# Statistics per token in four layer norms, one projection panel in each of them, and decay rows added on VectorE

## What is computed

```python
def _layer_norm(x, g, b):
    mu = jnp.mean(x, -1, keepdims=True)
    var = jnp.mean(jnp.square(x - mu), -1, keepdims=True)
    return (x - mu) * lax.rsqrt(var + NORM_EPS) * g + b

# _fox_attend, for 16 heads of layer 1 (log_f = log_sigmoid of a projection)
c = jnp.cumsum(log_f, axis=1)
s = einsum(q, k) * d ** -0.5 + c[query] - c[key]      # then causal mask, softmax, times v

# first_block, per layer i of 2
x = _layer_norm(DN_ALPHA * x + m, ln1_g[i], ln1_b[i])
x = _layer_norm(DN_ALPHA * x + _sq_relu_mlp(x, w_up[i], w_down[i]), ln2_g[i], ln2_b[i])
gate = jax.nn.sigmoid(x @ ple_w_gate[i] + ple_b_gate[i])
x = x + gate * (p[i] @ ple_w_proj[i])
```

## Time and profile before

| | us |
|---|---|
| median of 3 runs (lowest to highest) | 2610.25 (2610.14 to 2611.8) |
| the profiled execution, its own time | 2608.08 |
| its span, first to last instruction | 2606.2 |
| PE busy | 2520.6 (97%) |
| DVE, POOL, ACT busy | 1314.6, 1159.6, 923.9 |

### The profile page before, as it was taken

How to read it: one execution, slowest core, us unless ns; L and a number is a source line. 1 busy time by engine, 2 the same in 40 slices (tenths; PEclk the granted TensorE clock), 3 DMA queues, 4 the chain that set the end, 5 groups by cost and what they waited for, 6 DMA issues and landing times.

```text
span 2606.2 us, 47076 instructions
## 1 busy us (share of the span) xinstructions
PE 2520.6 (97%) x18452; PEld 2062.2 (79%) x18452; DVE 1314.6 (50%) x1952; ACT 923.9 (35%) x1479; POOL 1159.6 (44%) x688
## 2 busy tenths in 40 slices
PE   8899899999999998999999999999999999999997
PEld 6677688887787876888877888888888878788886
DVE  3655864346414258543466655566658873321113
ACT  4433422223623234222235333333345563432221
POOL 4444544444544445444445323333247744444442
PEclk9999999999999999999999999999999999999999
DMA  6211232232231212333322111111113223232331
GB/s 176 84 41 48 82 97 97 90 101 83 81 97 31 67 49 81 97 97 97 97 81 87 58 35 35 50 35 43 35 52 97 97 82 104 92 102 91 95 101 53
DMA packets 57721, 203.19 MB, mean 78 GB/s; under 512 B 6448, under 2 KB 9176, under 8 KB 57560
## 3 DMA queue, kind: packets, MB, share of 16 engines
q1 hardware_dynamic: 54288, 196.37, 23.5%
q10 hardware_dynamic: 2920, 3.44, 0.8%
q0 software_dynamic: 352, 1.05, 0.1%
HBM read 197.17 MB, written 3.67 MB: 77 GB/s over the span
## 4 chain that ended last, share of the span: by engine, by line
PE 89%; DVE 5%; ACT 2%; issue 1%; POOL 1%; DMA 0%; SPq 0%; DVEq 0%; ACTq 0%; POOLq 0%
PE banks L1936 24%; PE banks L1938 24%; PE banks L1937 24%; PE banks L2383 9%; PE banks L2151 1%; PE banks L2433 1%; PE banks L2134 1%; POOL sb_pa L1823 1%; DVE sb_x L1149 1%; PE banks L2069 1%; PE banks L2112 1%; PE banks L2108 1%; PE banks L2293 1%; ACT sb_pa L629 1%; PE banks L2284 1%
## 5 line engine op out<-in xcount | busy, mean ns | idle before, releaser
L1797 POOL TENSOR_TENSOR sb_wl<-sb_raw,sb_wh 128x1024 fp32r<-128x1024 f32 (+1 forms) x366 | 882.0, 2413 | 1052.8 <-ACT sb_wh L472 1052.5
L1936 PE MATMUL banks<-sb_bh,sb_wh 128*128 128x512 f32 x2656 | 1052.8, 396 | 47.4 <-POOL sb_bl L1809 24.0
L1938 PE MATMUL banks<-sb_bh,sb_wl 128*128 128x512 f32 x2656 | 1040.4, 392 | 0.0
L1937 PE MATMUL banks<-sb_bl,sb_wh 128*128 128x512 f32 x2656 | 1040.3, 392 | 0.0
L1936 PEld LDWEIGHTS banks<-sb_bh,sb_wh 128*128 128x128 f32 x2656 | 501.2, 189 | 173.0 <-issue 46.9
L1938 PEld LDWEIGHTS banks<-sb_bh,sb_wl 128*128 128x128 f32 x2656 | 500.9, 189 | 108.7
L1937 PEld LDWEIGHTS banks<-sb_bl,sb_wh 128*128 128x128 f32 x2656 | 501.5, 189 | 106.9 <-issue 2.2
L472 ACT CAST sb_wh<-sb_raw 128x1024 fp32r<-128x1024 f32 (+1 forms) x366 | 376.5, 1031 | 465.4 <-PE banks L1938 462.5
L2383 PEld LDWEIGHTS banks<-sb_m 64*64 64x64 f32 x5632 | 195.7, 134 | 16.6 <-issue 7.7
L1069 DVE SCALAR_TENSOR_TENSOR sb_x<-sb_x,banks 128x512 f32 x72 | 49.5, 687 | 314.9 <-PE banks L1938 314.9
L2383 PE MATMUL banks<-sb_m 64*64 64x64 f32 (+1 forms) x5632 | 206.7, 229 | 0.5 <-DVE sb_w L1586 0.2
(11 more groups left out here) (344 smaller groups left out, 2640.6 us busy)
## 6 DMA issues: line engine op xcount, KB each, us to landing
sb_raw<-w SPq DMA_DIRECT2D x366, 512.0 KB, 3.5
sb_x<-xT SPq DMA_DIRECT2D x4, 512.0 KB, 6.8
out<-sb_x SPq DMA_DIRECT2D x4, 512.0 KB, 2.6
bias_rows<-sb_brow ACTq DMA_DIRECT2D x1, 1536.0 KB
sb_pj<-pT POOLq DMA_DIRECT2D x2, 512.0 KB, 4.0
sb_t<-bias_rows ACTq DMA_DIRECT2D x1, 512.0 KB, 3.7
sb_sq<-bias_rows ACTq DMA_DIRECT2D x1, 512.0 KB, 4.7
sb_wm<-wm ACTq DMA_DIRECT2D x1, 288.0 KB, 3.0
```

Of the source, the lines that this page charges most:

```text
L1797: nc.gpsimd.tensor_tensor(wl[:, s, 0:cols], raw[:, s, 0:cols], wh[:, s, 0:cols].bitcast(F32), ALU.subtract).then_inc(lo_ready, 1)
L1936: nc.tensor.matmul(out, hi_a, hi_b, start=first, stop=False)
L1937: nc.tensor.matmul(out, hi_a, lo_b, start=False, stop=False)
L1938: return nc.tensor.matmul(out, lo_a, hi_b, start=False, stop=last)
```

## The change

**Norms.** The sums over channels are no longer spread over partitions. `tokens` puts 128 tokens at a time in the stationary place against two columns of ones, so each statistic comes out as one number per token, tokens on the partitions (128x2 for each of four token blocks). Mean, variance, root and reciprocal are computed on 8 or 16 columns. `along_tokens` brings mean and inverse root back to rows of 512 in banks 2 and 3 by products with the identity. A dummy root on ACT stands ahead of the real one. DVE subtracts the mean from x and writes the scaled chunk into a ring of PSUM banks 4 to 7. ACT adds the bias from there, once for the high part and once for x. Low parts of even chunks are now made by DVE (`low`), those of odd chunks by POOL (`norm_odd`). `filled_norm` puts one p projection panel (24 matmuls) into every norm, and `arriving` with two panels follows in norm 2 too. p is fetched after the attention and split in the output projection ahead of norm 1 (`ple_high`, `ple_low`).

**Decay.** The decay rows go to DRAM and come back spread over 128 partitions, 8 heads at a time (2 MB on ACT's queue, twice). The products with `fc_h` and `fc_l` are gone. DVE adds the row to the scores in place and takes the maximum in the same operation, negated; the exponential gets scale -1. The fetch of `fsel` and POOL's wait for it are gone.

The core of the diff:

```diff
-                dve.wait_ge(ln_dsq, w.ln + 1)
-                dve.wait_ge(ln_ss, w.ln + 1)
-                nc.vector.tensor_tensor(s1, psum[:, 3, :], sd, ALU.subtract).then_inc(ln_var, 1)
+                def scaled_x(c):
+                    if c >= 4:
+                        dve.wait_ge(nhi_ready, n0 + (c - 4 if c % 2 else c - 2))
+                    dve.wait_ge(ln_sub, m0 + c + 1)
+                    nc.vector.scalar_tensor_tensor(psum[:, 4 + c % 4, :], x[:, c, :], pcol(*gcol(c)), psum[:, 3, :],
+                                                   ALU.mult, ALU.mult).then_inc(t_ready, 1)
+                def low(c):
+                    dve.wait_ge(ln_hi, NC // 2 * w.ln + c // 2 + 1)
+                    nc.vector.scalar_tensor_tensor(bl[0][:, c, :], psum[:, 4 + c % 4, :], pcol(*bcol(c)),
+                                                   bh[0][:, c, :].bitcast(F32), ALU.add, ALU.subtract).then_inc(ln_low_even, 1)
...
+                nc.vector.reciprocal(tok_inv, tok_sd).then_inc(ln_inv, 1)
+                dve.wait_ge(ln_mean_spread, w.ln + 1)
                 less_mean(0)
                 less_mean(1)
-                dve.wait_ge(sd_ready, w.ln + 1)
-                link(nc.vector.reciprocal(rs, sd))
...
+            def filled_norm(layer):
+                pe.wait_ge(pl_ready, layer + 1)
...
+                        if t == 0 and k == 0:
+                            pe.wait_ge(ln_mean, w.ln)
+                            along_tokens(2, tok_mean).then_inc(ln_mean_spread, 1)
...
+                    if t == 0:
+                        pe.wait_ge(ln_inv, w.ln)
+                        along_tokens(3, tok_inv).then_inc(ln_inv_spread, 1)
...
-                pe.wait_ge(pl_ready, layer + 1)
-                short(4, ph, pl, 2)
-                short(4, ph, pl, 2)
-                panels(NC, 0, ready=(opnd_pool, w.op))
+                filled_norm(layer)
+                arriving(0, even_and_odd(w.op))
+                panels(NC - 2, 0)
...
+                            nc.vector.tensor_tensor_reduce(s_i, s_i, decay[:, 2 * u + e, 0:width], -1.0, -NEG,
+                                                           ALU.add, ALU.min, nm[:, ring, e:e + 1]).then_inc(nm_ready, 1)
...
-                    if kind == "fox":
-                        for part_of in (fc_h, fc_l):
-                            for e in range(2):
-                                pick = fsel_r[rows[e], chunk0 + u:chunk0 + u + 1].broadcast_to([64, P])
-                                nc.tensor.matmul(out[e], pick, part_of[rows[e], k_c], start=False, stop=False)
```

More of the change, by code:

```diff
@@ L522, in stream_norm, with ring, high @@
                 act.wait_ge(ln_var, w.ln + 1)
-                nc.scalar.activation(sd, s1, ACT.Sqrt, bias=eps[:, 0:1]).then_inc(sd_ready, 1)
+                nc.scalar.activation(tok_sd, tok_var, ACT.Sqrt, bias=eps[:, 0:1]).then_inc(sd_ready, 1)
+                def ring(c):
+                    return psum[:, 4 + c % 4, :]
+                def high(c):
+                    act.wait_ge(t_ready, NC * w.norm + c + 1)
+                    ins = nc.scalar.activation(bh[0][:, c, :], ring(c), ACT.Identity, bias=pcol(*bcol(c)))
+                    if c % 2 == 0:
+                        ins.then_inc(ln_hi, 1)
@@ new lines, in whole @@
+                def whole(c):
+                    if c % 2 == 0:
+                        act.wait_ge(ln_low_even, NC // 2 * w.ln + c // 2 + 1)
+                    nc.scalar.activation(x[:, c, :], ring(c), ACT.Identity, bias=pcol(*bcol(c))).then_inc(nhi_ready, 1)
+                projected(q, 0)
+                high(0)
+                projected(q, 1)
+                high(1)
+                whole(1)
+                projected(q, 2)
+                projected(q, 3)
+                whole(0)
@@ L524, in stream_norm @@
+                for c in range(2, NC, 2):
+                    high(c)
+                    high(c + 1)
+                    whole(c + 1)
+                    whole(c)
                 w.ln += 1
                 w.norm += 1
[L526 to L539, removed]
+                w.mid += 3
+                w.p += 1
+                w.g += 4
             def rms_square(c, slot):
@@ L1943, in bank_wait, with in_order, even_and_odd, ready @@
                     pe.wait_ge(bank_free[b], g.over2())
+            def in_order(sema, base):
+                return lambda k: pe.wait_ge(sema, base + k + 1)
+            def even_and_odd(op):
+                def ready(k):
+                    if k % 2:
+                        pe.wait_ge(opnd_pool, op + k // 2 + 1)
+                    else:
+                        pe.wait_ge(ln_low_even, NC // 2 * (w.ln - 1) + k // 2 + 1)
+                return ready
             def arriving(bo, ready, sums=lambda: None):
-                for j in range(2):
-                    pe.wait_ge(lo_ready, w.p + j + 1)
-                    bank_wait((w.g + j) % 2, Idx(0, w.g + j))
                 for k in range(NC):
@@ L2084, in panels_and_sums, with tokens, along_tokens @@
                 w.ln += 1
+            def tokens(b, at_, rows):
+                for tb in range(NB):
+                    out = psum[:, b, at_ + 2 * tb:at_ + 2 * tb + 2]
+                    last = nc.tensor.matmul(out, rows[:, tb * P:tb * P + P], ones[:, 0:2], start=True, stop=True, skip_group_check=True)
+                return last
+            def along_tokens(b, factors):
+                for tb in range(NB):
+                    f = factors[:, 2 * tb:2 * tb + 1].broadcast_to([P, P])
+                    last = nc.tensor.matmul(psum[:, b, tb * P:tb * P + P], f, ident[:, :], start=True, stop=True, skip_group_check=True)
+                return last
```

187 lines of the change are left out of this document (113 added, 74 removed).

## The result

The changed kernel takes 2598.38 us (median of 5 runs, 2594.52 to 2600.35), the kernel before 2610.25 (5 runs beside them, 2609.92 to 2611.8). The ratio is 0.995, 95% interval 0.9938 to 0.9961: 11.9 us faster, half of the forecast 23.5. A second set of 5 runs gave 2598.8. The profiled execution took 2600.35 us, the slowest of the first five, with a span of 2598.5.

The account below looks back on a forecast made before the run. PE, busy 97% of the span, was taken as the bound. Norms 22.0, sigmoid wait -2.8 and decay +4.3 summed to 23.5 us, from 2608.1 to 2584.6, median 2587 us; bounds 2580 to 2593, range 2579 to 2600.

Parts of the forecast that it names:

- rival 1: Norms: PE's clock falls during the small two-column sums, costing 6 to 16 us; 2596 us, chance 0.14.
- the 22.8 us of a norm: Each norm, from first small sum to the end of `arriving`, takes 22.8 us; two layers gain 22.0 (16 to 26).
- the decay's 4.3: Attention: PE saves 6.3 us by dropping decay products, DVE's longer maximum costs 2.0; net +4.3 us.
- the wait for chunk 7: End of each norm: PE gets the last chunk at 21.4 us after the sums start and ends at 22.8.
- Rival 3: Norms bound by DVE and ACT, not PE: each ends at 25.2 us, 10 less gained; 2597 us, chance 0.10.
- The new wait: Gate after norm 2: PE waits for the sigmoid to free bank 0, 2.1 us in layer 0, 0.7 in layer 1.
- Rival 2: Attention: DVE's fused add and maximum runs at half rate, net -5 us instead of +4.3; 2596 us, chance 0.12.
- the 2.0 that I took off for a slower maximum: Attention: DVE's maximum becomes a longer operation, costing 0.25 us for each of 8 head pairs, 2.0.
- PE saves 0.79 x 8: Attention: without decay products, only blocks 2 and 3 count, 0.79 us for each of 8 head pairs, 6.3.
- Rival 4: Attention: the decay rows come late through the DMA queues, making it slower; 2616 us or more, chance 0.04.
- Moved steps: Splitting p in the output projection, POOL's later fetch of p and the dropped `fsel` wait: taken as 0 us.

Follow-up runs that it names:

- sums_64_wide: The changed kernel with each small fp32 product of the norms' sums streaming 64 columns of ones instead of 2: 2588.73 us.
- sigmoid_first: The changed kernel with 64-column sums, layer 0's gate steps written out, a dummy sigmoid before the first wait and weight rounding after the first sigmoid: 2587.97 us.
- held_clock: The changed kernel with 64-column sums, layer 0's gate written out with the sigmoid first, and unread 512-column products in the attention: 2585.74 us.
- filled_waits: The changed kernel with 64-column sums and unread 512-column decay products where PE waits in the attention: 2586.13 us.

## Why the prediction was half right

The time, 2598.4, lies in the range of 2579 to 2600, at its end, and "faster" was right. The forecast of 2587 was 11.4 us off, and the likeliest case was not the one that came: rival 1 was, with a chance of 0.14. So the time is in the range because the range was drawn to cover the rivals, not because the sum was right: the forecast's own 2580 to 2593 misses it. Those bounds were also too narrow for the terms, which taken together (16 to 26, 0 to -5, -5 to 6.3) span 2578 to 2604. The step that failed is the clock: the 22.8 us of a norm, and the decay's 4.3, were reckoned at the full clock throughout.

- **The norms.** From the first small sum to the end of the two panels behind the norm (in norm 1 of layer 0, to the start of the next panel at 297.30 less its wait of 0.17), with the wait for the sigmoid left out:

| us | before | predicted | changed | sums_64_wide |
|---|---|---|---|---|
| norm 1, layer 0 | 26.0 | 22.8 | 26.4 | 23.2 |
| norm 2, layer 0 | 30.6 | 22.8 | 24.8 | 23.2 |
| norm 1, layer 1 | 26.0 | 22.8 | 26.4 | 23.2 |
| norm 2, layer 1 | 30.6 | 22.8 | 24.8 | 23.2 |
| sum | 113.2 | 91.2 | 102.4 | 92.8 |

  The kernel before has 24 matmuls fewer than the others in norm 1 and 24 more in norm 2, so the sums compare like with like. The gain was 10.8 instead of 22.0. The last column shows that the 22.8 was well built, 0.4 too short, and that what failed is the clock that it took for granted: (6.8 + 3.4 + 6.8 + 3.4) / 2 = 10.2 us. The details follow the clock too. In norm 2 of layer 0, where it fell later, the inverse was ready 4.9 after the start, as predicted; in norm 1 it took 5.7. The spread of the mean took 0.8 to the next record in sums_64_wide (predicted 0.86) and 1.56 in the changed kernel.
- **Rival 1.** The mechanism was right, the argument against it wrong. I wrote that the clock fell only in a wait and "stayed at 2.4 GHz in norm 2, where matmuls follow". But the sums of norm 2 were then four products of 512 columns, not 16 of 2. The stretch that I took as evidence did not hold what the change puts there. I also priced it at 6 us and it cost 10.2: the 2.5 us a norm came out (10.2 / 4), but I let the wait for chunk 7 hide 1.1 of it, and next to nothing was hidden (the two last columns of the table differ by 9.6).
- **Rival 3** did not come: PE is busy for 27.6 of 28 us, with waits of 0.2. DVE's operations were longer than I took them (0.68, 0.75 and 0.75 against 0.64, 0.70 and 0.70), and PE did not wait for them.
- **The new wait**: 2.2 and 0.7 measured, 2.1 and 0.7 predicted. The fall of the clock behind it (3.4 us, 1.7 lost) was not in the sum; it is not there after every such wait (see sigmoid_first).
- **The decay.** The work gained 6.0 us, predicted 4.3 (bounds -5 to 6.3). The term that was mis-sized is the 2.0 that I took off for a slower maximum: of PE's 6.3 some 0.3 were lost. Rival 2 did not come: with one source in PSUM the operation took 713 ns for 512 columns, not 1.2 us. The maxima of two heads take 0.70 + 0.73 + 0.14, partly overlapped: 1.40 us from start to end against 1.29, where I had 1.60. But the step "PE saves 0.79 x 8" had no clock in it either. In the new attention the clock fell 2 or 3 times a profile instead of 0 or 1, and alone the part was worth nothing.
- **Rival 4** did not come: 10.3 us to landing, and 43 were there. **Moved steps**: no wait for p or for its low part appeared.

The sum of the changed kernel's profile: -10.8 for the norms, +2.9 for the waits for the sigmoid and -6.0 for the decay give -13.9; four falls of 3.4 us that the profile of before does not have (at 143.7, 666.0, 932.2 and 1410.1) give back 6.8. Together -7.1; the profiled executions differ by 2608.08 - 2600.35 = 7.7. Of the four, the first stands ahead of everything that the change touches, where the profiles differ by chance (within the first 200 us the clock is low for 13.7 in the changed kernel and for 3.4 in held_clock). The last stands behind a wait of 2.0 us in the second block that the kernel before has too, without a fall. So only the two in the middle, 3.4 us, are tied to the change.

## What to carry to other kernels

A change that takes work from PE where PE is the bound is worth its full time only if the clock holds; look at what PE streams in the new stretch, and not only at whether it stands still. Eight records of 2 columns took nearly as long as eight of 64 (0.91 and 0.94 us, PEld busy for 0.97 in both), so widening them was nearly free here and bought 9.7 us. And before a stretch of the old profile is used as evidence on the clock, check that it has the same kind of instruction in it.

## What the runs showed of the hardware

- PE's clock fell while PE was issuing products without a gap: around 32 records on 2 columns, 3.6 us in all, it fell in all four norms of four profiles (in the changed kernel at 273.4, 2.7 us after the first record, and at 642.1, 4.0 after it, when the last had just been issued). With the same records on 64 columns it fell in none of 20 norms. I had expected falls only around idle stretches.
- In the attention with decay the clock fell 0 or 1 times a profile with the old products or as many, 2 or 3 times without them, and not at all with unread products in PE's waits.
- A kernel can gain clock with matmuls whose result nobody reads: 2.5 us more of rest, 6.0 less taken by the clock, the median 2.6 lower, near the limit of what can be told (filled_waits).
- The operation that adds a row from SBUF to scores in PSUM in place and takes the minimum took 713 ns for 512 columns, where a plain product on PSUM took 0.70 us, with a second instruction of 142 ns to fetch the result.
- 2 MB on ACT's queue, one source row to 128 partitions, landed in 10.3 us.
